# A transformer layer with expert retrieval on one core: the order of the output projection, and a fifth head of the second token block in the dense expert product

## What is computed

```python
x = x + gm_x * rms_norm(y_x, g_post_mix)         # y_x = [fourier, ssm] @ w_out, w_out 2048 x 2048
hx2 = modulate(rms_norm(x, g_pre_ffn), sf_x, cf_x)
y_f = peer_ffn(hx2, w_query, sub_keys_1, sub_keys_2, expert_u, expert_v)
x = x + gf_x * rms_norm(y_f, g_post_ffn)

def block(tb):                                    # peer_ffn: two blocks of 128 tokens
    q = (tb @ w_query).reshape(128, 8, 128)
    s1, s2 = q[..., :64] @ sub_keys_1.T, q[..., 64:] @ sub_keys_2.T   # per head, 128 keys each
    v1, i1 = top_k(s1, 16); v2, i2 = top_k(s2, 16)
    top_s, pos = top_k(v1[..., :, None] + v2[..., None, :], 16)       # of 256 pairs
    idx = (i1 * 128 + i2) at pos                  # 16 of 16384 experts per token and head
    act = gelu(einsum('td,thkd->thk', tb, expert_u[idx]))
    return einsum('thk,thkd->td', softmax(top_s) * act, expert_v[idx])
```

## Time and profile before

| | us |
|---|---|
| median of 3 runs | 1838.02 (1836.51 to 1843.12) |
| the profiled execution | 1832.72 |
| its span | 1830.9 |
| PE busy | 1457.1 (80%) |
| DVE busy | 1311.3 (72%) |
| POOL busy | 891.4 (49%) |
| ACT busy | 435.1 (24%) |
| moved | 683.72 MB, mean 373 GB/s |

### The profile page before, as it was taken

The page is one execution under the profiler, slowest core; times in us unless marked ns, Lnnn a source line. Parts: engine busy times, 40 slices in busy tenths (PEclk is TensorE's granted clock), DMA queues, the critical chain, the costliest instruction groups (busy, mean ns, idle before and its releaser), DMA issues.

```text
span 1830.9 us, 13641 instructions
## 1 busy us (share of the span) xinstructions
PE 1457.1 (80%) x4521; PEld 707.6 (39%) x4521; DVE 1311.3 (72%) x1684; ACT 435.1 (24%) x1160; POOL 891.4 (49%) x666
## 2 busy tenths in 40 slices
PE   5999999999999556655655666669999999989920
PEld 3434564575459312111111233345444444433300
DVE  3128877676138999999998787898556556556699
ACT  3012211120122222121223586687100000000000
POOL 0012233211006788888777787756455554322273
PEclk9999999999999766666667898979999999999965
DMA  9999989796658999999999999979999999999997
GB/s 364 378 361 342 352 334 326 300 348 244 221 186 345 380 418 420 418 418 420 419 419 417 405 406 391 381 291 386 414 413 412 413 413 413 381 418 417 417 422 312
DMA packets 164022, 683.72 MB, mean 373 GB/s; under 512 B 16433, under 2 KB 19057, under 8 KB 120689
## 3 DMA queue, kind: packets, MB, share of 16 engines
q0 software_dynamic: 92160, 503.36, 68.4%
q1 hardware_dynamic: 71360, 176.36, 25.5%
q10 hardware_dynamic: 432, 3.15, 0.4%
HBM read 678.51 MB, written 4.29 MB: 373 GB/s over the span
## 4 chain that ended last, share of the span: by engine, by line
DMA 35%; PE 28%; POOL 16%; DVE 14%; issue 5%; SPq 2%; ACT 0%; DVEq 0%; POOLq 0%; ACTq 0%
DMA arena<-in_expert_v,arena 27%; POOL arena L568 16%; DMA arena<-in_expert_u,arena 6%; PE PS L1807 6%; PE PS L1666 6%; PE PS L1567 5%; DVE arena L1382 5%; DVE arena L1425 3%; PE PS L1883 2%; DVE arena L1417 2%; PE PS L1548 2%; SPq L384 1%; PE PS L1523 1%; DMA arena<-in_w_mod 1%; DMA arena<-in_w_in 1%
## 5 line engine op out<-in xcount | busy, mean ns | idle before, releaser
L1382 DVE CUSTOM_DVE_ANT_0 arena<-arena 128x2048 f32<-128x2048 f32 x256 | 578.4, 2288 | 95.4 <-DMA arena<-in_expert_u,arena 94.4
L1883 PE MATMUL PS<-arena 128*128 128x512 f32 x512 | 364.1, 851 | 242.1 <-DMA arena<-in_expert_v,arena 242.0
L568 POOL DMA_INDIRECT arena<-in_expert_v,arena x256 | 401.9, 1570 | 285.8 <-DVE arena L1425 108.7
L568 POOL DMA_INDIRECT arena<-in_expert_u,arena x256 | 393.0, 1535 | 257.6 <-DVE arena L1357 89.5
L1935 PE MATMUL PS<-arena 128*128 128x512 f32 x1024 | 452.9, 600 | 16.3 <-DMA arena<-in_expert_v 14.2
L1935 PEld LDWEIGHTS PS<-arena 128*128 128x128 f32 x1024 | 192.7, 191 | 275.8 <-issue 227.4
L1883 PEld LDWEIGHTS PS<-arena 128*128 128x128 f32 x512 | 117.0, 253 | 456.4 <-DMA arena<-in_expert_v,arena 359.7
L1425 DVE SCALAR_TENSOR_TENSOR arena<-arena 128x2048 f32<-128x2048 f32 x62 | 145.8, 2351 | 56.9 <-DMA arena<-in_expert_v,arena 54.5
L1098 DVE SCALAR_TENSOR_TENSOR arena<-arena 128x1024 f32<-128x1024 f32 x120 | 160.9, 1341 | 25.7 <-DMA arena<-in_w_mod 22.9
L498 POOL DMA_DIRECT2D arena<-in_w_mod x128 | 68.8, 539 | 211.4 <-DVE arena L1098 180.7
L952 ACT ACTIVATE arena<-arena 128x4 f32<-128x4 f32 x64 | 13.0, 203 | 587.3 <-DVE arena L1382 516.2
(11 more groups left out here) (247 smaller groups left out, 1330.5 us busy)
## 6 DMA issues: line engine op xcount, KB each, us to landing
arena<-in_w_mod POOLq DMA_DIRECT2D x128, 512.0 KB, 7.3
arena<-in_expert_v SPq DMA_DIRECT2D x128, 512.0 KB, 8.0
arena<-in_w_mod SPq DMA_DIRECT2D x32, 1024.0 KB, 14.3
arena<-in_w_in SPq DMA_DIRECT2D x28, 1024.0 KB, 14.4
arena<-in_w_out SPq DMA_DIRECT2D x16, 1024.0 KB, 12.9
arena<-in_w_query SPq DMA_DIRECT2D x8, 1024.0 KB, 8.5
arena<-in_x SPq DMA_DIRECT2D x4, 1024.0 KB, 6.1
arena<-cum_rows SPq DMA_DIRECT2D x4, 1024.0 KB, 10.0
```

Source lines behind the costliest of these rows:

```text
L568: nc.gpsimd.indirect_dma_start(slot, None, table, bass.IndirectOffsetOnAxis(ap=rows[:, n:n + 1], axis=0),).then_inc(arrived, 16)
L1382: V.tensor_tensor_reduce(out=rows, in0=rows, in1=h2row[u // PH], scale=1.0, scalar=0.0, op0=ALU.mult, op1=ALU.add, accum_out=dots[:, u % B ...
L1883: ins = M(PS[:, b, :], diag_slot[m % DIAGS], slot[:, b * NQ:(b + 1) * NQ], start=(m == 0), stop=(m == BLK - 1))
```

## The change

Two things. **Projection:** the order becomes (0,0), (1,0), (2,0), (3,0), (2,1), (3,1), (0,1), (1,1); behind (2,1) PE makes the h2 transposes of block 0, query 0 and its scores, and DVE picks the first index and begins with the dots; x1 and h2 of block 1 stand behind dots 9 and 10, with the routing of unit 1. Panels 0 and 1 of w_out are loaded a second time, and the first 128 columns of w_query also into a place of their own. The first 32 U gathers use the early slots (the first 12 of them four, then five). **Dense product:** `DENSE = UNITS - 3`, so block 1's heads 0 to 4 are in it. 16 more U dots come before it; the fifth head's 16 slots are stacked for four groups of tokens on 128 partitions, so there are 24 batches in 8 quarters, each quarter one batch of the fifth head and two of the other four, and each part of G takes two matmuls. 40 pairs and 48 whole rows are left for the items. V's gathers, the routing and the places of `close(0)` and of the right half's addition are placed anew. The core of the diff:

```diff
-U_EARLY = 20
+U_EARLY, EARLY_FEW = 32, 12
+EARLY_OF = [n % 4 if n < EARLY_FEW else (n - EARLY_FEW) % EARLY for n in range(U_EARLY)]
...
-DENSE = UNITS - 4
+DENSE = UNITS - 3
 N_DENSE = DENSE * TOPK
-LEFT = N_DENSE - BLK
+LEFT = BLK // 2
+MAIN = BLK + LEFT
 BATCH = 4
 BATCHES = P // BATCH
-STACKED = BATCHES // 2
+QUARTERS = BATCHES // 4
+STACKED = 3 * QUARTERS
...
-V_POS = [20 + 110 * m // 62 if m < 62 else 130 + 57 * (m - 62) // 50 for m in range(V_EARLY)] + [187, 188, 190, 191]
+V_POS = [40 + 90 * m // 62 if m < 62 else 130 + 73 * (m - 62) // 50 for m in range(V_EARLY)] + [203, 204, 206, 207]
...
-ROUTE_AT = {16 + 49 * (r - 2) // 4: r for r in range(2, UNITS)}
-ITEMS = [("u", N_DENSE + i) for i in range(20)]
-ITEMS += [x for i in range(LEFT // 2) for x in (("pair", BLK + 2 * i), ("u", N_DENSE + 20 + i))]
-ITEMS += [("u", N_DENSE + 20 + LEFT // 2 + i) for i in range(44 - LEFT // 2)]
-ITEMS += [("full", N_DENSE + i) for i in range(4 * TOPK)]
-FEW, MANY = 15, 88
+T_AT, T_ACT, DUP_AT, T_MORE, T_MORE_ACT = 134, 130, 194, 204, 203
+ROUTE_AT = {16 + 53 * (r - 2) // 4: r for r in range(2, UNITS)}
+ITEMS = [("u", N_DENSE + i) for i in range(28)]
+ITEMS += [x for i in range(20) for x in (("pair", BLK + 2 * i), ("u", N_DENSE + 28 + i))]
+ITEMS += [("pair", BLK + 2 * i) for i in range(20, (N_DENSE - BLK) // 2)]
+ITEMS += [("full", N_DENSE + i) for i in range(3 * TOPK)]
+FEW, MANY = 15, 84
 RING_OF = [k % 3 if k < FEW else (0, 1, 3, 4)[(k - FEW) % 4] if k < MANY else (0, 1, 3, 4, 5, 6, 7, 8)[(k - MANY) % 8] for k in range(len(ITEMS))]
-RING_BASE = [16 * U_EARLY // EARLY] * 5 + [16 * ((N_DENSE - U_EARLY + NU - 1) // NU)] * 4
+RING_BASE = [16 * EARLY_OF.count(s) for s in range(EARLY)] + [16 * ((N_DENSE - U_EARLY + NU - 1) // NU)] * 4
 ROWS = [m for kind, i in ITEMS for m in {"u": [], "pair": [i, i + 1], "full": [i]}[kind]]
-GAIN_AT, CLOSE_AT, RIGHT_AT = 124, len(ITEMS) - 16, len(ITEMS) - 8
+GAIN_AT, CLOSE_AT, RIGHT_AT = 112, len(ITEMS) - 6, len(ITEMS) - 3
 TAILS, MORE_TAILS = 4, 8
...
-        + [("out", n * NQ) for n in range(4)]
+        + [("out", n * NQ) for n in (0, 1, 2, 3, 0, 1)]
         + [("query", n * NQ) for n in range(2)])
-R_XBC, R_FZ, R_OUT, R_QUERY = 0, 3, 7, 11
...
-OUT_ORDER = [(0, 0), (0, 1), (1, 0), (1, 1), (2, 0), (3, 0), (2, 1), (3, 1)]
+OUT_ORDER = [(0, 0), (1, 0), (2, 0), (3, 0), (2, 1), (3, 1), (0, 1), (1, 1)]
+OUT_DONE = [4, 8]
+OUT_LAST_USE = [1, 2, 5, 6, 7, 8]
...
-ROWS_AT = (2, 0)
-SUMS_AT = {(1, 0): 6, (1, 1): 7}
-H2T_AT = 4
-EXP_AT = 3
+ROWS_AT = (3, 0)
+SUMS_AT = {(1, 0): 6, (2, 0): 7}
+H2T_AT = 7
+EXP_AT = 7
 KEYS_AFTER, PAIRS_AFTER = 1, 5
-FIRST_KEYS_AFTER, FIRST_PAIRS_AFTER, FIRST_WEIGHTS_AFTER = 4, 9, 3
-WEIGHTS_AFTER = 15
+SECOND_X1_AFTER, SECOND_ROW_AFTER = 9, 10
+FIRST_WEIGHTS_AFTER = {3: 0, 22: 1, 40: 2}
...
-                    sp.wait_ge(wo_ps, OUT_ORDER.index((i - R_OUT, 1)) + 1)
+                    sp.wait_ge(wo_ps, OUT_LAST_USE[i - R_OUT])
...
-            for j in range(R_OUT + 2, R_QUERY):
-                ring_load(j)
+            ring_load(R_OUT + 2)
+            sp.wait_ge(y_ps, 2)
+            sp.dma_start(first_query, w_query.rearrange("(k p) n -> p k n", p=P)[:, :, 0:P]).then_inc(mid_in, 16)
+            ring_load(R_OUT + 3)
...
-            for j in range(R_QUERY, len(RING)):
+            for j in range(R_OUT + 4, len(RING)):
                 ring_load(j)
...
-                    sp.wait_ge(g_ps, 2 * BATCHES - 4)
-                elif i == 2:
                     sp.wait_ge(g_ps, 2 * BATCHES)
...
-                    if n == EARLY - 1:
+                    s = EARLY_OF[n]
+                    if s in EARLY_OF[:n]:
+                        pool.wait_ge(u_used, max(m for m in range(n) if EARLY_OF[m] == s) + 1)
+                    elif s == EARLY - 1:
                         pool.wait_ge(h2_ready, 2)
-                    if n >= EARLY:
-                        pool.wait_ge(u_used, n - EARLY + 1)
-                    gather(expert_u, early[n % EARLY], early_in[n % EARLY], n)
+                    gather(expert_u, early[s], early_in[s], n)
...
+                if (n, t) == (2, 1):
+                    h2T_out(0)
+                    q_out(0)
+                    scores_out(0)
+                if (n, t) == (3, 1):
+                    softmax_exp(0)
             y_norm(1)
...
+            for u in range(1, UNITS):
+                q_out(u)
+                if u == 1:
                     x1_norm(1)
+                else:
+                    scores_out(u - 1)
...
-            for b in range(STACKED):
-                if b + 3 < STACKED:
-                    first_halves_stacked(b + 3)
-                if V_LATE + 2 + b < BLK:
-                    diagonal(V_LATE + 2 + b)
-                g_out(BATCHES + 2 * b)
-                g_out(BATCHES + 2 * b + 1)
+            for e in range(QUARTERS):
+                if e + 1 < QUARTERS:
+                    first_halves_stacked(3 * e + 3)
+                for b in (2 * e, 2 * e + 1):
+                    if V_LATE + 2 + b < BLK:
+                        diagonal(V_LATE + 2 + b)
+                    g_out(BATCHES + 2 * b)
+                    g_out(BATCHES + 2 * b + 1)
+                if e + 1 < QUARTERS:
+                    first_halves_stacked(3 * e + 4)
+                    first_halves_stacked(3 * e + 5)
...
-                dve.wait_ge(wo_evac, OUT_ORDER.index((3, t)) + 1)
+                dve.wait_ge(wo_evac, OUT_DONE[t])
...
             pick_keys(0)
-            x1_variance(1)
             pick_pairs(0)
-            h2_make(1)
             for n in range(N_DENSE):
                 dot(n)
+                if n == SECOND_X1_AFTER:
+                    x1_make(1)
+                if n == SECOND_ROW_AFTER:
+                    x1_variance(1)
+                    pick_keys(1)
+                    pick_pairs(1)
+                    h2_make(1)
                 if n in weights_after:
                     weights(weights_after[n])
...
+                    elif q == 0:
+                        pe.wait_ge(rows_evac, 2)
...
+                if u:
+                    ring_wait(j)
+                else:
+                    pe.wait_ge(mid_in, 48)
...
-                if t == 0:
+                if (n, t) in OUT_ORDER[:4]:
                     ring_wait(R_OUT + n)
-                if n >= 2:
-                    pe.wait_ge(wo_evac, OUT_ORDER.index((n - 2, t)) + 1)
+                elif n < 2:
+                    ring_wait(R_OUT + 4 + n)
+                before = [i for i in range(OUT_ORDER.index((n, t))) if OUT_ORDER[i][1] == t and OUT_ORDER[i][0] % 2 == n % 2]
+                if before:
+                    pe.wait_ge(wo_evac, before[-1] + 1)
...
-                elif (n, t) == (0, 1):
-                    w_out(0, 1, FOURIER, stop=False)
+                elif (n, t) == (1, 0):
                     pe.wait_ge(yt_evac, 2)
-                    ins = w_out(0, 1, SSM, start=False)
+                    ins = w_out(n, t, FOURIER + SSM)
...
+                if (n, t) == (2, 1):
+                    h2_transposes(0)
+                    query(0)
+                    pe.wait_ge(keys_in, 32)
+                    key_scores(0)
+
+            for u in range(1, UNITS):
                 query(u)
-                if u == 0:
-                    pe.wait_ge(keys_in, 32)
-                if u != 1:
-
-                    key_scores(max(u - 1, 0))
+                if u > 1:
+                    key_scores(u - 1)
                 if u == H2T_AT:
                     h2_transposes(1)
...
+            def scatter_stacked(e, r):
+
+                last, q = 3 * e, 3 * e + 1 + r
+                pe.wait_ge(oh_dve, BATCHES + 2) if q == 1 else pe.wait_ge(oh_act, BATCHES + q - 1)
+                pe.wait_ge(oh2_dve, q + 1)
                 for h in range(2):
-                    bank_free(BATCHES + 2 * b + h)
-                    part = slice(h * LEFT, (h + 1) * LEFT)
+                    bank_free(BATCHES + 4 * e + 2 * r + h)
+                    part, rows = slice(h * LEFT, (h + 1) * LEFT), slice(32 * (2 * h + r), 32 * (2 * h + r) + TOPK)
                     for i in range(BATCH):
-                        ins = M(PS[:, 6 + h, i * P:(i + 1) * P], oh1[b % 4][part, i, :], oh2[b % 5][part, i, :], start=True, stop=True)
+                        to = PS[:, 6 + h, i * P:(i + 1) * P]
+                        M(to, oh1[q % 4][part, i, :], oh2[q % 5][part, i, :], start=True, stop=False)
+                        ins = M(to, oh1[last % 4][rows, i, :], oh2[last % 5][rows, i, :], start=False, stop=True)
                     ins.then_inc(g_ps, 1)
...
-            for b in range(STACKED):
-                scatter_stacked(b)
-                if V_LATE + b < BLK:
-                    early_rows(V_LATE + b)
+            for e in range(QUARTERS):
+                for r in range(2):
+                    scatter_stacked(e, r)
+                    if V_LATE + 2 * e + r < BLK:
+                        early_rows(V_LATE + 2 * e + r)
```

169 lines of the change are left out of this document (88 added, 81 removed).

## The result

The changed kernel takes 2017.36 us (median of four runs, 2011.11 to 2021.70), the kernel before 1839.68 beside it (1836.51 to 1843.12): a ratio of 1.096, 95% interval 1.092 to 1.100, or 178 us more. The forecast was 1877 with a range of 1830 to 1898. The direction was right, the size was not. The profiled execution took 2011.11 us, its span is 2009.3 us and the mean granted clock 0.859.

What follows compares the result with a forecast made beforehand. Limits by stage: TensorE in the projection, transfers from 541 to 1219 us, both in the dense product. 28 + 40 + 28 + 3 + 1 - 59 = +41 on 1832.7 gave 1873.7, 1879 on the median; taken 1877, range 1830 to 1898.

Steps and rivals of the forecast that it cites:

- (ii): Stacked scatter: 24 batches for 16, eight more by 3.5 us, +28 us, bounds +20 and +35.
- The front: Reordered projection, reloads and early gathers: 12 MB or 28 us late by 695 us, range 17 to 36.
- Step 1: Projection unit (2,0) waits for ACT's copy of (0,0): 25 us stall (14 to 28), plus 3 us at lower clock.
- step 3: Reloaded w_out panel 1 beside gathers gets a third, 0.139 MB/us: landed at 578, 18 us stall.
- Index 0: First routing index, behind the transposes and query 0: there at 542.5 us, 13.4 earlier.
- rival C: Reload of panel 1 starves, one turn per row, 0.084 MB/us: lands at 590, total 1888; chance 0.14.
- the even share of 2 KB and 4 KB rows: Projection: 2 KB panels beside 4 KB modulation tiles got about equal bytes; held against the starved reload.
- Dot 11: First U dot needing block 1's routing and h2: put at 626 us.
- (i): Before the dense product: sixteen more rows of U, 16.8 MB, delay its start by +40 us.
- (iii): V's rows spread wider between dots 130 and 203: +3 us, 0 to 8.
- (iv): Dense product: same 128 tiles, 50 for 44 in the eight-slot stretch, +1 us, between -24 and +6.
- (v): Behind the dense product: 20 us for 79.4 before, -59 us, range -60 to -50.

Runs made afterwards that it cites:

- experiment 4: The changed kernel, but the first matmul of each stacked-scatter pair also takes the second's 16 rows: 1942.4 us.
- the scatter in turn: The kernel before plus only the fifth unit, scatter matmuls alternating halves (64, 64, 16, 16 rows): 1877.8 us, ratio 1.022.

## Why the prediction was wrong

**The step that failed is (ii), the stacked scatter**, and in it one term: "PE has 32 matmuls a step for 16, 1.71 us twice". The count was right, the price was not. It carried 0.107 us a record from the earlier trace rows, where all matmuls have 64 rows, to a sequence that changes between 64 and 16 rows each time. The two groups of after, PE's share of the stage by line (busy us, mean ns of a record with its overlap, idle before):

```profile
L1985 PE MATMUL PS<-arena 64*128 64x128 f32 x256 | 92.4, 458 | 19.5 <-issue 17.0 <-ACT arena L966 2.5
L1986 PE MATMUL PS<-arena 16*128 16x128 f32 x256 | 92.2, 456 | 0.0
```

That is 184 us, and would take 512 x 0.107 = 55 by that price. 256 changes by 0.20 make 51 of the difference; the other 79 are the clock, which stood at 0.56. How much of the low clock comes from the 16-row matmuls is not shown (experiment 4). With the matmuls at 6.6 us a step even at full clock, PE alone set the pace, and the question that the step did ask (DVE's 10.2 us a quarter against PE's 10.7) was beside the point. The stage grew by 168 us instead of 28.

The same step was too low in its other half as well. With the 16-row matmuls left out, or made cheap, the stage is still 106.5 or 101.9 us, 4.4 and 4.2 us a batch for 3.5. Of the chain of the latter from 1314 to 1416 us, 34.7% are its scatter matmuls, 14.3% ACT's halves of the one-hot matrices (L964), 8.9% the row matmuls and 6.8% ACT's copies (L973). I did not take this apart further.

**The front**: forecast +28 (17 to 36), measured +36.9 alone, just outside. The waits were those forecast, and two of their sizes were off. Step 1, the stall of (2,0) with the half clock behind it, and step 3, the panel:

```profile
453.69 1.84 PE L1643 MATMUL PS<-arena 128*128 128x1 f32 x16
474.20 16.77 PE L1850 MATMUL PS<-arena 128*128 128x512 f32 x32 [18.67 <-ACT arena L839]
...
492.51 13.98 PE L1850 MATMUL PS<-arena 128*128 128x512 f32 x32
...
588.82 15.80 PE L1850 MATMUL PS<-arena 128*128 128x512 f32 x32 [33.80 <-DMA arena<-in_w_out]
```

PE stood 18.7 us for the forecast 25 (from 455.5 to 474.2, forecast 453.4 to 478), and the unit behind it took 2.8 us more than the next (forecast 3). Index 0 was there at 537.9 for 542.5. Step 3 was mis-sized, by the share: the panel landed at 588.8 and not at 578, and the stall was 33.8 us for 18. From 541 to 588.8 its 4.19 MB came at 0.088 MB per us, a fifth of the 0.418 that all transfers have, and not a third. That is rival C's price (landed at 590), which I gave 0.14. I had set the even share of 2 KB and 4 KB rows against it, and that reading was wrong. Those three tiles of before were the last, and from 457 to 464.2 us their queue moved 413 packets to the panel's 697: it had not always a row waiting, as I read it now. In after, where both queues had work (445 to 460 us), packets went 1070 to 1066 and the 2 KB rows got a third of the bytes, not half. So one law, a row for a row, mis-sized both steps: the tiles were done 5 us before the forecast and the panel came 11 us behind it. Dot 11 came at 630 for 626. By 695 us 77.5 MB had moved for 93.7 due (121 x 0.214 + 154 x 0.335), 16.2 MB or 39 us, against 12 MB and 28. The experiment with the gathers held shows the share as the cause of PE's wait, and that the 2 KB rows behind it are next.

**(i) and (iii)**: 40 + 3 forecast for the start of the scatter. With the fifth unit alone the first stacked matmul starts at 1266.5 us for 1223.8, 42.7 late.

**(iv)**: the dense product is 10 us shorter for +1, within its bounds of -24 to +6. Of the 29 us that before had over its 439 of matmuls, 44 tiles at 3.78 us for 3.43 explain 15, and the step carried the rest over; after has 19, of which 50 such tiles explain 17.5. **(v)**: 20.0 us behind it, as forecast; -59 is what the change really brings.

**The sum again, with what was measured**: 37 + 43 + 168 - 10 - 59 = +179, for the span's +178. The error of 137 us is 140 in (ii) and 9 in the front, less 11 in the dense product. With 28 in (ii), as forecast, the sum would be +39 for +41, in part by errors that cancel. That the change is slower was rightly forecast, but 140 of the 178 us are a cost that the forecast did not have. No rival had it: the highest price of the scatter in any of them was +28, and the range went to +35. For a resource in a new pattern (a matmul of another size between two of the old) the trace of before had no row, and the step should have said so and bounded it; a price seen only in an unbroken run of one kind is such a bound from below. The Trainium skill's sentence on the drain (TensorEngine Tiling (Array Packing), Tiling Modes) was there to read and stood against this very step.

**Is there a version that beats both?** Not among those tried. With the scatter in turn the fifth unit costs 42 us, with no change of size at all, where G gets terms of other tokens, 26; the front with the gathers held costs 28. What the change wins, 59 us behind the dense product, is paid for by 40 us of rows ahead of it and at least 42 us of batches.
